# RMSNorm gains off the DMA queue: norm2 as a column product, final_norm as one row repeated by TensorE

## The reference, cut to what matters

```python
def _rmsnorm(x, gain):
    xf = x.astype(jnp.float32)
    return xf * lax.rsqrt(jnp.mean(xf * xf, axis=-1, keepdims=True) + NORM_EPS) * gain

    x = x + merged @ w_out
    x = x + _hier_moe(_rmsnorm(x, norm2), router_group, ..., exp_gate, exp_up, exp_down)
...
y_prompt = _rmsnorm(hp, final_norm)
y_sample = _rmsnorm(hs, final_norm)
```

## Time and profile before

| what | value |
|---|---|
| median of 3 runs | 816.77 us (816.7 to 818.26) |
| the profiled execution | 820.28 us |
| its span, first to last instruction | 818.5 us |
| granted TensorE clock, mean of the span | 0.984 |
| PE / DVE / ACT / POOL busy | 94% / 52% / 31% / 9% |
| bytes moved by DMA | 162.37 MB |

### The profile page before, as it was taken

The page is one execution under the profiler, slowest core; times in us unless marked ns, Lnnn a source line. Parts: engine busy times, 40 slices in busy tenths (PEclk is TensorE's granted clock), DMA queues, the critical chain, the costliest instruction groups (busy, mean ns, idle before and its releaser), DMA issues.

```text
span 818.5 us, 18378 instructions
## 1 busy us (share of the span) xinstructions
PE 765.5 (94%) x7164; PEld 476.8 (58%) x7164; DVE 426.5 (52%) x1137; ACT 255.8 (31%) x619; POOL 73.7 (9%) x85
## 2 busy tenths in 40 slices
PE   4999999999999999999999899998899999988884
PEld 4666666666666666666666664454555555544441
DVE  3364677778767867777687746245113211111116
ACT  4224353452443433534524523221111111111112
POOL 3000000400000000000000000001222222212110
PEclk9999999999999999999999989999999999999997
DMA  9553161870251341610703715978999999999975
GB/s 224 128 128 73 28 163 36 156 188 11 61 155 26 82 113 26 158 37 26 188 11 94 300 33 197 385 291 329 312 387 385 387 385 382 391 377 394 392 306 195
DMA packets 117638, 162.37 MB, mean 198 GB/s; under 512 B 27973, under 2 KB 92279, under 8 KB 110920
## 3 DMA queue, kind: packets, MB, share of 16 engines
q1 hardware_dynamic: 100852, 149.14, 54.0%
q0 software_dynamic: 5968, 8.54, 4.3%
q10 hardware_dynamic: 10773, 4.06, 1.9%
HBM read 156.00 MB, written 15.73 MB: 210 GB/s over the span
## 4 chain that ended last, share of the span: by engine, by line
PE 79%; SPq 7%; DMA 6%; ACT 2%; DVE 2%; issue 2%; POOL 0%; ACTq 0%; POOLq 0%; DVEq 0%
PE bank L788 23%; PE bank L1196 9%; PE bank L959 5%; PE bank L1093 4%; PE bank L1203 4%; PE bank L794 4%; PE bank L1037 4%; SPq L552 3%; DMA shared<-in_exp_up 3%; PE bank L1189 3%; SPq L555 2%; PE bank L892 2%; PE bank L760 2%; PE bank L901 2%; SPq L583 1%
## 5 line engine op out<-in xcount | busy, mean ns | idle before, releaser
L788 PE MATMUL bank<-xnT,wall 128*128 128x320 f32 x656 | 196.7, 444 | 2.4 <-ACT vecs L1372 2.4
L788 PEld LDWEIGHTS bank<-xnT,wall 128*128 128x128 f32 x656 | 119.2, 190 | 49.3 <-issue 5.5
L2133 DVE SCALAR_TENSOR_TENSOR vecs<-vecs,bank 128x128 f32<-128x128 f32 x32 | 9.2, 287 | 129.3 <-ACT vecs L1596 126.5
L2129 DVE COPY vecs<-bank 128x512 f32<-128x512 f32 x32 | 22.1, 691 | 58.1 <-PE bank L1203 44.2
L959 PE MATMUL bank<-xnT,wall 128*128 128x320 f32 x128 | 47.9, 456 | 0.3
L1596 ACT ACTIVATE vecs<-bank 128x128 f32<-128x128 f32 x32 | 8.9, 277 | 121.9 <-PE bank L1196 121.9
L1196 PE MATMUL bank<-scratch 128*64 128x256 f32 x320 | 39.8, 405 | 6.6 <-DMA scratch<-in_exp_up 5.4
L1196 PE MATMUL bank<-vecs,scratch 128*64 128x256 f32 x352 | 40.4, 382 | 5.8 <-DMA vecs<-in_exp_up 5.0
L683 POOL DMA_INDIRECT merged<-xn2d,gidx x4 | 3.7, 917 | 416.0 <-DVE gidx L2085 415.1
L1189 PEld LDWEIGHTS bank<-consts_sb,merged 64*128 64x128 f32 x240 | 28.7, 199 | 13.8 <-issue 13.8
L689 POOL DMA_INDIRECT ybuf<-vecs,sidx x30 | 30.4, 1015 | 69.9 <-DVE vecs L2129 69.3
(11 more groups left out here) (420 smaller groups left out, 1359.3 us busy)
## 6 DMA issues: line engine op xcount, KB each, us to landing
wall<-in_w_in SPq DMA_DIRECT2D x58, 512.0 KB, 5.9
vecs<-in_exp_gate SPq DMA_DIRECT2D x11, 1024.0 KB
vecs<-in_exp_up SPq DMA_DIRECT2D x11, 1024.0 KB
scratch<-in_exp_gate SPq DMA_DIRECT2D x10, 1024.0 KB
scratch<-in_exp_up SPq DMA_DIRECT2D x10, 1024.0 KB
scratch<-in_exp_down SPq DMA_DIRECT2D x6, 1024.0 KB
shared<-in_exp_gate SPq DMA_DIRECT2D x10, 512.0 KB
shared<-in_exp_up SPq DMA_DIRECT2D x10, 512.0 KB
```

Of the source, the lines that this page charges most:

```text
L788: q = mm(tpbank(L, name), wbuf[name][:, k, :], xnT[:, k, :], start=(k == 0), stop=(k == KC - 1))
L2129: CP(ye[:, e % 2, :], bank[6 + e % 2][:]).then_inc(S("ye"), 1)
```

## The change

`norm2` is no longer multiplied into `xn2`: DVE's `plain(t)` writes x times the inverse root. The gain comes in where the rows stand transposed: there a gain is one number for each partition and column block, and a small tile `n2` [128, 8], loaded by POOL at the start, is multiplied in by DVE while it copies the PSUM bank to `xgT`. These copies leave ACT. `final_norm` is loaded by ACT at the start as 8 more rows of `murows` (43 rows now); during the experts 14 and 16 PE multiplies a one-hot row of the identity, repeated over 128 columns, by `murows`, which puts one row of 128 gains on all 128 partitions of a PSUM bank, 4 matmuls for each half; ACT copies each half to `fnb`, and at expert 30 makes the two halves `fnh` from it. The six broadcast DMAs of SP (L572, L576 twice, L629, L632 twice) and SP's wait are gone. The semaphore `slotT` is now `late` and counts these copies too.

```diff
         vrows = sb("vrows", [P, P])
-        murows = sb("murows", [NMU + KC, P])
+        NROWS = NMU + 2 * KC
+        murows = sb("murows", [NROWS, P])
+        n2 = sb("n2", [P, KC])
...
-            sp.dma_start(norm2b, a["norm2"].broadcast_to([P, D])).then_inc(S("x1_in"), 16)
             for h in range(2):
                 c = slice(512 * h, 512 * h + 512)
                 sp.dma_start(x1h[at64(h), :], a["x_sample"].rearrange("b t d -> (b t) d")[:, c]).then_inc(S("x1_in"), 16)
-                sp.dma_start(norm2h[at64(h), :], a["norm2"][:, c].broadcast_to([64, 512])).then_inc(S("x1_in"), 16)
...
-            sp.wait_ge(S("gu"), LAST_OF[3] + 1)
-            sp.dma_start(fnb, a["final_norm"].rearrange("(a d) -> a d", a=1).broadcast_to([P, D])).then_inc(S("fn_in"), 16)
-            for h in range(2):
-                src = a["final_norm"].rearrange("(a d) -> a d", a=1)[:, 512 * h:512 * h + 512]
-                sp.dma_start(fnh[at64(h), :], src.broadcast_to([64, 512])).then_inc(S("fn_in"), 16)
-
...
+            pool.dma_start(n2[:], a["norm2"].rearrange("o (p k) -> p (o k)", k=KC)).then_inc(S("rt_in"), 16)
...
-                pe.wait_ge(S("st_in"), 16 * 6)
+                pe.wait_ge(S("st_in"), 16 * 7)
...
+            def final_gains(part):
+
+                if part:
+                    pe.wait_ge(S("late"), 3)
+                for c in range(4):
+                    r = NMU + KC + 4 * part + c
+                    q = mm(bank[5][:, P * c:P * c + P], ident[0:NROWS, r:r + 1].broadcast_to([NROWS, P]), murows[:], start=True, stop=True)
+                q.then_inc(S("late_ps"), 1)
...
+                if e == 14:
+                    pe.wait_ge(S("late"), 2)
+                    final_gains(0)
+                if e == 16:
+                    final_gains(1)
...
+            act.dma_start(murows[NMU + KC:, :], a["final_norm"].rearrange("(c p) -> c p", p=P)).then_inc(S("st_in"), 16)
...
-            def xcols(b):
-                A(xgT[:, b], bank[b][:].rearrange("p (k s) -> p k s", k=KC), ACT.Copy).then_inc(S("gT"), 1)
-
...
-            for j in range(2):
-                act.wait_ge(S("gT_ps"), j + 1)
-                A(xgT[:, 0:2, 4 * j:4 * j + 4, :].rearrange("p b k s -> p k b s"),
-                  bank[4 if j else 1][:].rearrange("p (k b s) -> p k b s", k=4, b=2), ACT.Copy).then_inc(S("gT"), 1)
...
-                if 2 <= e < NE - 1:
-                    next_cols(e + 1)
...
-                if e == 1:
-                    next_cols(2)
+                if e in (14, 16):
+                    part = (e - 14) // 2
+                    act.wait_ge(S("late_ps"), 3 + part)
+                    A(fnb[:, 512 * part:512 * part + 512], bank[5][:], ACT.Copy).then_inc(S("late"), 1)
+                if e == NE - 2:
+                    act.wait_ge(S("late"), 4)
+                    for h in range(2):
+                        A(fnh[at64(h), :], fnb[at64(h), 512 * h:512 * h + 512], ACT.Copy).then_inc(S("late"), 1)
...
-            dve.wait_ge(S("x1_in"), 16 * 6)
+            dve.wait_ge(S("x1_in"), 16 * 3)
...
+            def plain(t):
+
+                dst, x = (xn2h, x1h) if t == 2 else (xn2[:, t, :], x1[:, t, :])
+                TS(dst, x, rowst[:, 6 + t:7 + t], None, MUL).then_inc(S("xn2"), 1)
+
...
-                scale(t, norm2h if t == 2 else norm2b, "xn2")
+                plain(t)
...
+            for j in range(2):
+                dve.wait_ge(S("gT_ps"), j + 1)
+                for b in range(2):
+                    q = TT(xgT[:, b, 4 * j:4 * j + 4, :], bank[4 if j else 1][:].rearrange("p (k b s) -> p k b s", k=4, b=2)[:, :, b, :],
+                           n2[:, 4 * j:4 * j + 4, None].broadcast_to([P, 4, CAP]), MUL)
+                q.then_inc(S("gT"), 1)
...
+            def gained(bank_cols, e):
+
+                dve.wait_ge(S("gT_ps"), e + 1)
+                TT(xgT[:, e % 2], bank_cols.rearrange("p (k s) -> p k s", k=KC), n2[:, :, None].broadcast_to([P, KC, CAP]), MUL).then_inc(S("gT"), 1)
...
+                if 1 <= e < NE - 1:
+                    gained(bank[(e + 1) % 2][:], e + 1)
                 if e:
                     outputs(e - 1)
...
-            dve.wait_ge(S("fn_in"), 48)
+            dve.wait_ge(S("late"), 6)
```

More of the change, by code:

```diff
@@ L403, in hawk_rwkv7_moe @@
         dup = late[:, 640:1408].rearrange("p (t e c) -> p t e c", t=3, e=ON_CHIP)
+        fnb = consts[:, CONST["blk"][0] + 640:CONST["blk"][0] + 640 + D]
         gate2 = [vrows, vT]
@@ L753, in states @@
                     tr(bank[1][0:w, 8 * c:8 * c + 8], shrows[:, c * P:c * P + w], ident[0:8, 0:8])
-                tr(bank[2][:, 256:256 + NMU + KC], murows[:], ident[0:NMU + KC, 0:NMU + KC]).then_inc(S("vecT"), 1)
+                tr(bank[2][:, 256:256 + NMU + KC], murows[0:NMU + KC, :], ident[0:NMU + KC, 0:NMU + KC]).then_inc(S("vecT"), 1)
             pe.wait_ge(S("xnT"), 6)
@@ L1249, in slot_rows @@
                 else:
-                    pe.wait_ge(S("slotT"), 1)
+                    pe.wait_ge(S("late"), 1)
                     for x in range(ON_CHIP):
                         q = tr(bank[5][:, 64 * x:64 * x + 64], dup[0:64, 2, x, :], ident[0:64, 0:64])
-                q.then_inc(S("slotT_ps"), 1)
+                q.then_inc(S("late_ps"), 1)
[5 more added lines that the diff above has]
+                    q = mm(bank[5][:, P * c:P * c + P], ident[0:NROWS, r:r + 1].broadcast_to([NROWS, P]), murows[:], start=True, stop=True)
+                q.then_inc(S("late_ps"), 1)
             def hot_out(x):
@@ L1282, in _ @@
                     slot_rows(e // 2 - 5)
+                if e == 14:
[3 more added lines that the diff above has]
+                    final_gains(1)
             dn(NE - 1)
-            pe.wait_ge(S("slotT"), 2)
+            pe.wait_ge(S("late"), 4)
             hot_out(0)
@@ L1323, in _ @@
             act.dma_start(murows[26:27, 0:32], a["rwkv_mu"][:, 26 * P:RWKV]).then_inc(S("st_in"), 16)
-            act.dma_start(murows[NMU:, :], a["norm2"].rearrange("o (c p) -> (o c) p", p=P)).then_inc(S("st_in"), 16)
+            act.dma_start(murows[NMU:NMU + KC, :], a["norm2"].rearrange("o (c p) -> (o c) p", p=P)).then_inc(S("st_in"), 16)
+            act.dma_start(murows[NMU + KC:, :], a["final_norm"].rearrange("(c p) -> c p", p=P)).then_inc(S("st_in"), 16)
             act.wait_ge(S("first_in"), 16)
@@ L1608, in _ @@
                 with act.Fori(0, NOV) as j:
-                    act.wait_ge(S("gT_ps"), j + (NE + 1))
-                    A(xgT[:, 0], bank[7][:].rearrange("p (k s) -> p k s", k=KC), ACT.Copy).then_inc(S("gT"), 1)
                     act.wait_ge(S("gu"), j + (NE + 1))
@@ L1980, in inverse @@
                 step(nc.vector.reciprocal(rowst[0:n, 6 + t:7 + t], rowst[0:n, 3 + t:4 + t]))
+            def plain(t):
+                dst, x = (xn2h, x1h) if t == 2 else (xn2[:, t, :], x1[:, t, :])
+                TS(dst, x, rowst[:, 6 + t:7 + t], None, MUL).then_inc(S("xn2"), 1)
             def scale(t, gains, sem):
[L1984 to L1988, removed]
+                x = x1h if t == 2 else x1[:, t, :]
+                STT(x, x, rowst[:, 6 + t:7 + t], gains, MUL, MUL).then_inc(S(sem), 1)
             def logits(t):
                 step(STT(lg[:, t, :], bank[4 if t == 2 else 5][:, 64 * t:64 * t + NG + NE], rowst[:, 6 + t:7 + t], rb[:], MUL, ADD))
-            dve.wait_ge(S("rt_in"), 16 * 5)
+            dve.wait_ge(S("rt_in"), 16 * 6)
             TT(rw[:], rw[:], muT[:, NMU:, None].broadcast_to([P, KC, NG + NE]), MUL).then_inc(S("rw_n"), 1)
@@ L2116, in slot_columns @@
             def slot_columns(part):
-                dve.wait_ge(S("slotT_ps"), part + 1)
+                dve.wait_ge(S("late_ps"), part + 1)
                 if part == 0:
-                    CP(late[:, 0:512], bank[5][:]).then_inc(S("slotT"), 1)
+                    CP(late[:, 0:512], bank[5][:]).then_inc(S("late"), 1)
                 else:
-                    CP(late[:, 512:640], bank[5][:, 0:128]).then_inc(S("slotT"), 1)
+                    CP(late[:, 512:640], bank[5][:, 0:128]).then_inc(S("late"), 1)
             def outputs(e):
@@ L2150, in _ @@
                 with dve.Fori(0, NOV) as j:
+                    dve.wait_ge(S("gT_ps"), j + (NE + 1))
+                    TT(xgT[:, 0], bank[7][:].rearrange("p (k s) -> p k s", k=KC), n2[:, :, None].broadcast_to([P, KC, CAP]), MUL).then_inc(S("gT"), 1)
                     dve.wait_ge(S("th"), j + (NE + 1))
```

5 lines of the change are left out of this document (removed).

## The result

The changed kernel takes 810.14 us (median of 7 runs, 808.91 to 813.73), the one before 817.07 (7 runs, 816.63 to 821.57). The ratio is 0.9915, its 95% interval 0.9893 to 0.9937.

What follows compares the result with a forecast made beforehand. The prediction took the expert weight stream, 558 to 791 us at 377 GB/s, as the bound with PE in slack; all terms 0 except final_norm's -0.4, and the profiled-to-median difference of 3.5 gave 816.4 us, range 814.5 to 818.2.

Steps and rivals of the forecast that it cites:

- The likeliest forecast: Whole kernel: 816.4 us, 0.4 less at the last scatter and nothing elsewhere; chance 0.64, own range 815.6 to 817.2.
- A: Tail: the final_norm broadcast holds up scatter and first `ybuf` loads in full; end 2.1 us earlier, 814.7; chance 0.20.
- B: Expert stream: it follows PE after all, so PE's delay reaches the end; 817.9 to 819.3 us; chance 0.12.
- C: Before the stream: dropping norm2's broadcast gains 2.1 us, 814.3; sign: stream starts before 557 us; chance 0.04.
- The stream is the bound, PE has slack: 558 to 791 us: weight loads at share 1.01 and 377 GB/s set the time; PE could be 8 us late unnoticed.
- The first transposed rows on DVE: +0.45: Stream's start: four DVE products replace ACT's copies, making PE's first product, at 560.68 us, 0.3 to 0.6 us later.
- final_norm by PE: 0.9 for eight matmuls: Experts 14 and 16: eight PE matmuls of 128 columns cost 0.9 us together, priced from four transposes at 0.44 us.
- PE's 1.5 us in all, 0 at the end: Stream: PE's delays of 0.45 + 0.2 + 0.9 us are covered by queued weights and PE's later waits; end unmoved.
- the forecast 0.2 for the later copies: Experts 2 and 3: PE waits 0.09 us more each for DVE's copy of the transposed rows, 0.2 in all.
- The lull before the stream: Just before SP's first stream load at 558.09 us: four microseconds with the DMA engines 17% busy.
- norm2 not broadcast: 0: At 508 us: 768 KB less lets DVE start about 2 us earlier, but PE notices nothing; gain nothing.
- final_norm: -0.4, within 0 to 0.7: Kernel's end: 768 KB less lets the last scatter land 0.4 us earlier, and `ybuf` loads and combines move up equally.

Runs made afterwards that it cites:

- the pad alone: The kernel before with only an unused tile of 8 floats (32 bytes per partition) allocated where the change allocates `n2`: 810.81 us, ratio 0.9917.
- the change without the shift: The changed kernel with `n2` allocated last, so every other tile starts where it did before: 818.63 us against 817.33 for the kernel before, ratio 0.9993.
- the second execution: The kernel before, unedited, profiled once more: 816.55 us, span 814.7, stream from 554.12 us, granted clock 1.00 in the mixers.
- the other pairs: Kernels with and without the change; one pair has all weight tiles at multiples of 256 bytes: 810.15 us with the change, 810.81 without.

## Why the prediction was wrong

**The step that failed** is in the part on what bounds the kernel: "the time is set by when the stream starts, by its bytes, and by what follows it". I took the rate of the stream, 377 GB/s at a share of 1.01, for a constant of the chip. A share of one says that each engine always has a packet, not that a packet can't be shorter. The rate belonged to this layout: 54.2 MB in 150 us with the buffers at 224 mod 256, 55.8 with them at 0. And in going through the change I priced each operation and each load but not the line `n2 = sb(...)`, which executes nothing. It has no price of its own and moves the start of each weight buffer. Its term in the sum should have been nearly the whole result: -6.1 us of stream (225.2 to 219.1) of the 6.9, shown by the pad alone at 0.9917 and by the change without the shift at 0.9993.

**No rival had it.** The likeliest forecast, A, B and C share the fixed rate, so the range rested on the wrong assumption from end to end. A list of tile starts before and after the change, taken modulo 256, would have put a rival there. With one transaction more for each row of 4 or 8 KB off the boundary, "DMA: Bandwidth & Descriptors" of the Trainium skill ("How a descriptor splits into AXI transactions") gives, as an estimate of mine, 3 to 6% for the stream: 225 us would have become 212 to 218, if all of the buffers moved. The measured 219.1 is a little above.

**The terms of the sum, one by one.**

- *The stream is the bound, PE has slack.* Right. The changed kernel has a DMA share of 1.02 from 600 to 750 us, PE's first product comes later at the stream's start (next point), and with the shift taken out the time stays.
- *The first transposed rows on DVE: +0.45.* From PE's line L1166 (before L1172) to the first product it was 560.68 - 558.70 = 1.98 us, and is 556.32 - 554.01 = 2.31: +0.33. The four products took 1.42, forecast at 1.4.
- *final_norm by PE: 0.9 for eight matmuls.* Mis-sized: 1.16 + 1.15 = 2.3 us. The price was taken from four transposes (0.44 us). The four products of a half are eight records in the trace (`x8`, L1255), where the four transposes are four.
- *PE's 1.5 us in all, 0 at the end.* The sum is nearer to 2.8 (0.33 + 2.3, and the forecast 0.2 for the later copies). The 0 at the end is right all the same, by the change without the shift: ratio 0.9993. PE's slack covered the error.
- *The lull before the stream.* The window of 556 to 560 us at 17% reaches 2 us beyond SP's issue at 558.09; from 554 to 558 the share is 0.56, from 556 to 558 it is 0.09. No term hangs on it.
- *norm2 not broadcast: 0.* Right in place and size: DVE waits 2.6 us less (7.74 against 10.38; 2.4 against the 10.16 of the second execution), and the change without the shift shows no gain.
- *final_norm: -0.4, within 0 to 0.7.* The scatter gained more than its range, 6.16 to 5.17 here, 5.97 to 5.01 and 6.17 to 5.43 in the other pairs. That "the loads from `ybuf`, the combines and the rest move up by it one for one" isn't borne out: the last load from `ybuf` is 0.4, 0.8 and 0.9 us longer in these pairs, and net it is 15.62 - 15.05 = 0.6, 15.18 - 14.97 = 0.2 and 15.47 - 15.61 = -0.14 us. These differences are smaller than the spread of that stretch among the executions without the change, 14.50 to 17.98. So the 0.6 near the forecast 0.4 is luck, and whether the change lengthens the load wasn't tried.
- *Rival A, the tail in full (2.1 us).* Its sign, a scatter that lands in 4 us or a shorter load, is not there. *Rival B,* PE's delay reaching the end: not there either. *Rival C:* what it looked for, a stream that starts before 557 us, did appear, at 553.40, and mostly for another reason, the granted clock of the profiled execution: the kernel before starts its stream at 554.12 where its clock is 1.00. A sign stated as a time on the axis of one execution could be met by the clock alone; it should have been stated as a distance.

## What to carry to other kernels

A DMA share of one is a bound on time, not on bytes: where a stream of large loads bounds a kernel, look at where its destination tiles start, and try them at multiples of 256 bytes in their partition first: it costs a pad, and was worth 0.8% here. An edit that adds or resizes a small tile moves all tiles behind it, so compare the starts before and after, and when such an edit gives a surprising gain or loss, run the old kernel with only a pad of the same size. And compare the new kernel with the old one at equal starts, or the layout's gain is booked to the idea: here the idea was worth nothing that can be measured, the 32 bytes 0.8%.

## What the hardware showed that I had not expected

- The start of the destination in SBUF, modulo 256 bytes, changes the rate of HBM to SBUF loads with rows of 2 to 8 KB under full load by 3.0% (54.19 to 55.80 MB in 150 us on q1). 64 and 128 mod 256 are no better than 224 (54.35 and 54.50 MB); 256 mod 512 is as good as 0 (55.76).
- Loads with short rows lose more of their DMA time: the same 12868 packets and 8.04 MB of the first 50 us, mostly rows of 512 bytes, take 68.3% of the engines' time with `wall` off the boundary and 59.6% on it. PE's busy time there stays the same, so that isn't where the kernel's gain comes from.
- The gain grows with the bytes that are aligned and then stops: 5.5 of 18 MB made 3.7 us by the ratio, 13 made 6.8, all 18 made 6.4 in the kernel before and 7.4 in the change.
- With 768 KB less behind it in the queue, the last scatter lands 0.7 to 1.0 us sooner in three pairs of kernels. That part of the change alone wasn't run, so the cause is argued and not shown.
